# A decoder layer on one core: half of a gate block loaded inside the conditioning stream, a weight split moved ahead of a convolution, and one head's gathers reordered

## What is computed

```
mod = silu(c) @ w_ada + b_ada            # 6 x 2048: sh1, sc1, gt1, sh2, sc2, gt2
h = x * (1 + sc1) + sh1
proj = h @ w_in                          # splits: xr 2048, gr 2048, q_c 512, kv_c 512, k_r 64, g_rnn 2048, g_mla 2048
y_rnn = rg_lru(conv4(xr), gates) * gelu(gr) @ w_rnn_out
y_mla = attention(rms_norm(q_c), rms_norm(kv_c), rope(k_r)) @ w_mla_out     # 16 heads
x = layer_norm(a * x + (1 + gt1) * ((sig(g_rnn) * y_rnn + sig(g_mla) * y_mla) @ w_o))
h = x * (1 + sc2) + sh2
q = h @ peer_wq;  top 16 of 16384 experts for each of 8 heads and each token
y = sum_k gelu(h . expert_u[i_k]) * g_k * expert_v[i_k]
x = layer_norm(a * x + (1 + gt2) * y)
```

## Time and profile before

| | us |
|---|---|
| median of 3 runs | 2333.32 |
| the profiled execution's own time | 2334.12 |
| its span | 2332.4 |
| PE busy | 2073.0 (89%) |
| DVE busy | 1483.1 (64%) |
| ACT busy | 578.9 (25%) |
| POOL busy | 765.9 (33%) |
| data moved | 807.81 MB, mean 346 GB/s |

### The profile page before, as it was taken

One profiled execution on the slowest core, in us unless ns is written; L12 is line 12 of the kernel. 1 busy time (PEld: TensorE's weight loads), 2 busy tenths in 40 slices (PEclk: granted clock), 3 DMA queues, 4 the chain that ended last, 5 costly groups with the idle time before them and its releaser, 6 DMA issues.

```text
span 2332.4 us, 23238 instructions
## 1 busy us (share of the span) xinstructions
PE 2073.0 (89%) x7716; PEld 1346.1 (58%) x7716; DVE 1483.1 (64%) x2123; ACT 578.9 (25%) x1113; POOL 765.9 (33%) x764
## 2 busy tenths in 40 slices
PE   4899999999999999999987887788888899888987
PEld 3788999977888887788433333333333333333433
DVE  5746767868877556579366646665666667465444
ACT  1012553563343333221121111111111111112011
POOL 0000000011110000045465555554554554555562
PEclk7899999999999999999999889988899988989998
DMA  9976767766998675779999999999999999999996
GB/s 353 386 226 213 249 221 248 240 230 229 382 344 282 206 253 180 251 299 409 368 422 421 422 422 422 422 422 422 422 421 421 421 422 421 421 421 422 421 423 272
DMA packets 215881, 807.81 MB, mean 346 GB/s; under 512 B 24797, under 2 KB 45941, under 8 KB 149493
## 3 DMA queue, kind: packets, MB, share of 16 engines
q0 software_dynamic: 92160, 604.02, 63.5%
q1 hardware_dynamic: 122984, 202.05, 25.3%
q10 hardware_dynamic: 656, 0.66, 0.1%
HBM read 804.57 MB, written 2.10 MB: 346 GB/s over the span
## 4 chain that ended last, share of the span: by engine, by line
PE 54%; DMA 18%; DVE 11%; POOL 6%; issue 6%; ACT 4%; SPq 1%; POOLq 0%; DVEq 0%; ACTq 0%
PE ps L563 53%; DMA front<-in_peer_u,arena 15%; DVE front L1955 4%; DVE arena L1456 2%; POOL arena L504 2%; POOL front L496 1%; DMA front<-in_w_ada 1%; POOL arena L496 1%; DMA front<-in_peer_v,arena 1%; DMA arena<-in_peer_v,arena 1%; POOL arena L484 1%; POOL front L504 1%; SPq L339 1%; DMA arena<-in_w_in 1%; DVE arena L1862 0%
## 5 line engine op out<-in xcount | busy, mean ns | idle before, releaser
L563 PE MATMUL ps<-arena 128*128 128x512 f32 (+5 forms) x2798 | 967.0, 499 | 221.8 <-ACT arena L1268 182.5
L563 PEld LDWEIGHTS ps<-arena 128*128 128x128 f32 (+1 forms) x2798 | 515.5, 207 | 655.5 <-issue 467.5
L1955 DVE CUSTOM_DVE_ANT_0 front<-front,arena 128x2048 f32<-128x2048 f32 x180 | 409.3, 2292 | 199.6 <-DMA front<-in_peer_u,arena 195.5
L563 PE MATMUL ps<-front,arena 128*128 128x512 f32 (+1 forms) x832 | 355.9, 577 | 2.0 <-DMA front<-in_peer_v,arena 2.0
L1955 DVE CUSTOM_DVE_ANT_0 arena<-arena 128x2048 f32<-128x2048 f32 x60 | 137.5, 2294 | 266.2 <-DMA arena<-in_peer_u,arena 265.4
L496 POOL DMA_INDIRECT front<-in_peer_u,arena x176 | 248.5, 1412 | 68.3 <-issue 44.8
L563 PEld LDWEIGHTS ps<-front,arena 128*128 128x128 f32 x832 | 157.4, 190 | 191.1 <-issue 186.2
L1256 ACT ACTIVATE arena<-arena 128x4 f32<-128x4 f32 x64 | 13.2, 207 | 906.4 <-DVE arena L1935 906.2
L1609 DVE TENSOR_TENSOR split_ring<-front,split_pada 128x2048 fp32r<-128x2048 f32 x72 | 165.0, 2291 | 111.5 <-ACT split_pada L1147 111.1
L484 POOL COPY arena<-arena 128x4 uint32 (+1 forms) x120 | 78.2, 652 | 375.1 <-PE ps L563 350.9
L455 POOL DMA_DIRECT2D arena<-in_w_ada x64 | 34.2, 535 | 491.7 <-DVEq L1521 198.4
(11 more groups left out here) (273 smaller groups left out, 2580.8 us busy)
## 6 DMA issues: line engine op xcount, KB each, us to landing
front<-in_w_in SPq DMA_DIRECT2D x68, 1024.0 KB, 7.6
arena<-in_w_ada POOLq DMA_DIRECT2D x128, 512.0 KB, 6.2
front<-in_w_ada SPq DMA_DIRECT2D x64, 512.0 KB, 7.8
front<-in_w_rnn_out SPq DMA_DIRECT2D x16, 1024.0 KB, 6.7
front<-in_w_mla_out SPq DMA_DIRECT2D x16, 1024.0 KB, 5.2
front<-in_w_o SPq DMA_DIRECT2D x16, 1024.0 KB, 5.1
front<-in_peer_wq SPq DMA_DIRECT2D x11, 1024.0 KB, 9.8
arena<-in_w_ukv SPq DMA_DIRECT2D x16, 512.0 KB, 5.8
```

What stands on the lines that cost most here:

```text
L563: return pe.matmul(o, l, r, start=start, stop=stop, skip_group_check=True, **k)
L1955: V.tensor_tensor_reduce(uslot[s], uslot[s], h2[T], 1.0, 0.0, ALU.mult, ALU.add, zraw[:, s:s + 1]).then_inc(dots_done, 1)
```

## The change

Three parts, and two orders on ACT that belong to the first.

1. *Half a gate block in the stream.* Columns 0 to 255 of the gr block are loaded in four 512 KB pieces (`half_w`), each behind the three early units of its round, and run as `early_half(j)`, 8 matmuls into PSUM bank 5. For that the one-column sums (`ada_columns`) and the rotation of k_r move to bank 4, and stand ahead of the half. The ring then brings only columns 256 to 511, and `unit(B_XR + 1, s)` has 8 matmuls in place of 16. ACT copies the half out behind the stream, makes the square roots next and the high part of `hT` only then; the first two weights of the heads may be split earlier.
2. *First attention weights.* DVE's `head_weight(0)` moves ahead of `convolve(0)`.
3. *Third head.* The four U groups of round 2 are taken out of the loop and stand ahead of `v_group(0, 2)`, `(0, 3)`, `(1, 0)` and `(1, 1)`; the loop begins at round 2.

```diff
                 if j >= 2:
+                    sp.wait_ge(halves_used, j - 1)
+                sp.dma_start(half_w[j % 2], wv["w_in"][:, 4 * j:4 * j + 4, C_GR:C_GR + 256]).then_inc(in_head[j % 2], 16)
...
-                sp.dma_start(ring3[s], wv["w_in"][:, 4 * s:4 * s + 4, C_GR:C_GR + 512]).then_inc(in_ring[s], 16)
+                sp.dma_start(ring3[s][:, :, 256:512], wv["w_in"][:, 4 * s:4 * s + 4, C_GR + 256:C_GR + 512]).then_inc(in_ring[s], 16)
...
-            for q in (2, 3):
-                v_group(0, q)
+            for q in range(TOPK // GROUP):
+                u_group(1, 1, q)
+                v_group(*((0, q + 2) if q < 2 else (1, q - 2)))
+            v_group(1, 2)
+            v_group(1, 3)
             last = NT * PH - 1
-            with pool.Fori(1, last - 2) as H:
-                me.enter(H, 1, 2 * TOPK // GROUP)
+            with pool.Fori(2, last - 2) as H:
+                me.enter(H, 2, 2 * TOPK // GROUP)
...
-                    for m in range(4):
+                    for m in (2, 3):
                         last = mm(o[:, m, :], ring3[s][:, k, m * P:(m + 1) * P], hT[:, kt, :], kt == 0 and m % 2 == 0, kt == KT - 1)
...
+            def early_half(j):
+
+                pe.wait_ge(in_head[j % 2], 16 * (j // 2 + 1))
+                for k in range(4):
+                    kt = 4 * j + k
+                    for m in range(2):
+                        last = mm(ps[:, 5, m * S:(m + 1) * S], half_w[j % 2][:, k, m * P:(m + 1) * P], hT[:, kt, :], kt == 0 and m == 0, kt == KT - 1)
+                last.then_inc(halves_used, 1)
...
+                if j < 3:
+                    ada_columns(j + 1)
+                    early_half(j)
             last.then_inc(kr_done, 1)
             early_unit(3, 2)
+            early_half(3)
...
             low_channels(0)
+            head_weight(0)
             convolve(0)
-            head_weight(0)
```

More of the change, by code:

```diff
@@ L199, in build @@
         krw = at3(R_OT, KT, 2 * ROPE)
+        half_w = [infront(R_MODS + 3 * D + 1024 * i, 1024).rearrange("p (t c) -> p t c", t=4) for i in range(2)]
         ada_acc = at(W + 9216, 1024)
@@ L280, in build @@
         in_early = [sem(f"in_early{i}") for i in range(6)]
+        halves_used = sem("halves_used")
         in_ada = [sem(f"in_ada{i}") for i in range(3)]
@@ L303, in build @@
         keys_t, keys_ok = sem("keys_t"), sem("keys_ok")
-        var_ok, std1_ok, h2_ok, h2T_done, h2T_out = (sem(n) for n in ("var_ok", "std1_ok", "h2_ok", "h2T_done", "h2T_out"))
+        var_ok, std1_ok, h2T_done, h2T_out = (sem(n) for n in ("var_ok", "std1_ok", "h2T_done", "h2T_out"))
         sc_done, sc_out, stage_ok, best_ok, gexp_ok, topk_ok, zero_ok = (sem(n) for n in (
@@ L350, in _ @@
                     sp.dma_start(early_w[3 * (j % 2) + c], wv["w_in"][:, 4 * j:4 * j + 4, col:col + 512]).then_inc(in_early[3 * (j % 2) + c], 16)
+                if j >= 2:
+                    sp.wait_ge(halves_used, j - 1)
+                sp.dma_start(half_w[j % 2], wv["w_in"][:, 4 * j:4 * j + 4, C_GR:C_GR + 256]).then_inc(in_head[j % 2], 16)
                 if j == 0:
@@ L528, in _ @@
                     v_group(H, q)
-            me.leave(last - 3)
+            me.leave(last - 4)
             u_group(last - 1, 0, 0)
@@ L586, in unit, with ada_columns @@
                     kt = 4 * s + k
-                    for m in range(4):
+                    for m in (2, 3):
                         last = mm(o[:, m, :], ring3[s][:, k, m * P:(m + 1) * P], hT[:, kt, :], kt == 0 and m % 2 == 0, kt == KT - 1)
                 last.then_inc(unit_used, 1)
+            def early_half(j):
[5 more added lines that the diff above has]
+                last.then_inc(halves_used, 1)
+            def ada_columns(j):
+                pe.wait_ge(acc_ok, j + 1)
+                for h in range(2):
+                    for k in range(4):
+                        o = S + 8 * j + 4 * h + k
+                        last = mm(ps[:, 4, o:o + 1], acc[:, j, h, k * P:(k + 1) * P], ones[:, 0:1], j == 0 and h == 0 and k == 0, True)
+                last.then_inc(modc_done, 1)
             def early_unit(j, c):
@@ L602, in _ @@
             pe.wait_ge(xT_out, KT // 2)
+            ada_columns(0)
             for j in range(4):
[L604 to L608, removed]
                 pe.wait_ge(hT_ok, 4 * j + 4)
@@ L613, in _ @@
                 for kt in range(4 * j, 4 * j + 4):
-                    last = mm(ps[:, 4, 0:S], krw[:, kt, :], hT[:, kt, :], kt == 0, kt == KT - 1)
+                    last = mm(ps[:, 4, 0:S], krw[:, kt, :], hT[:, kt, :], False, kt == KT - 1)
+                if j < 3:
+                    ada_columns(j + 1)
+                    early_half(j)
             last.then_inc(kr_done, 1)
             early_unit(3, 2)
+            early_half(3)
             pe.wait_ge(kr_out, 1)
-            mm(ps[:, 5, 0:S], cst[:, K_ROT:K_ROT + P], krraw, True, True).then_inc(krot_done, 1)
+            mm(ps[:, 4, 0:S], cst[:, K_ROT:K_ROT + P], krraw, True, True).then_inc(krot_done, 1)
             for i in range(2):
@@ L629, in _ @@
             for g in range(4):
-                if g == 2:
+                if g == 1:
                     pe.wait_ge(std_ok, 2)
@@ L646, in queries @@
                 b = h % 2
-                pe.wait_ge(in_head[b], 32 * (h // 2 + 1))
+                pe.wait_ge(in_head[b], 32 * (h // 2 + 2))
                 if h and h % 4 == 0:
@@ L1043, in _ @@
             channels_out(B_XR, infront(XR, 1024))
-            act.wait_ge(hT_ok, KT)
-            A(S_HT[0], at(S_HT[2], KT * S), ACT.Copy).then_inc(shi_ok, 1)
+            act.wait_ge(halves_used, 4)
+            A(infront(GR, 512), ps[:, 5, :], ACT.Copy)
             for i in range(2):
@@ L1048, in _ @@
                 A(rs2[i], ps[:, 6 + i, 0:S], ACT.Sqrt, bias=eps_rms, scale=1.0 / RANK).then_inc(std_ok, 1)
+            act.wait_ge(hT_ok, KT)
+            A(S_HT[0], at(S_HT[2], KT * S), ACT.Copy).then_inc(shi_ok, 1)
             for g in range(4):
@@ L1055, in head_weight @@
                 act.wait_ge(in_ring[s], 16 * (b + SLOT_BASE))
-                act.wait_ge(unit_used, 4 * b + s - 1)
+                if i == 0:
+                    act.wait_ge(q_done, 4)
+                else:
+                    act.wait_ge(unit_used, 4 * b + s - 1 if i > 1 else 4 * B_XR + 5)
                 if i == 26:
@@ L1066, in _ @@
             head_weight(1)
-            channels_out(B_XR + 1, infront(GR, 1024))
+            act.wait_ge(unit_used, 4 * (B_XR + 2))
+            A(infront(GR + 512, 512), ps[:, 3, :], ACT.Copy).then_inc(out_act, 1)
             def output(h):
@@ L1463, in _ @@
                 dve.wait_ge(xT_out, KT // 2)
-                me.do(TT(sh1, ps[:, 5, 0:4], modc[:, 4 * j:4 * j + 4], ALU.add))
-                me.do(TT(sc1, ps[:, 5, 4:8], modc[:, KT + 4 * j:KT + 4 * j + 4], ALU.add))
+                me.do(TT(sh1, ps[:, 4, S + 8 * j:S + 8 * j + 4], modc[:, 4 * j:4 * j + 4], ALU.add))
+                me.do(TT(sc1, ps[:, 4, S + 8 * j + 4:S + 8 * j + 8], modc[:, KT + 4 * j:KT + 4 * j + 4], ALU.add))
                 me.wait()
@@ L1482, in _ @@
             me.do(TT(rt, krraw, cosT, ALU.mult))
-            me.do(TT(krT, ps[:, 5, 0:S], sinT, ALU.mult))
+            me.do(TT(krT, ps[:, 4, 0:S], sinT, ALU.mult))
             me.wait()
```

## The result

| | before | after |
|---|---|---|
| median, us | 2333.84 (5 runs, 2332.66 to 2338.18) | 2348.04 (5 runs, 2346.64 to 2355.31) |
| the profiled execution | 2334.12 | 2355.31 |
| its span | 2332.4 | 2353.6 |

The changed kernel takes 1.0061 times as long (95% interval 1.0045 to 1.0076): it is **slower by some 14 us**, where 11 us less were forecast.

The account below looks back on a forecast made before the run. It took PE's dense stretch up to the experts, then DMA at 422 GB/s, as the bounds. Stream -4.0 and POOL -6.9 gave -10.9: 2323.2 us for the profiled execution, 2322.4 as median, range 2317.5 to 2328.

Parts of the forecast that it names:

- The stream, -4.0 forecast: PE's entry into the heads: 4.7 for three half loads, 1.8 and 3.5 for halves on PE, -14.0 from ring units.
- the second edit: First head weight split ahead of the convolution: avoids 3.3 us of PE waiting for DVE, and nothing beyond.
- POOL, -6.9 forecast: Start of the experts: U gathers issued earlier fill the 25 us from 1125 that ran at 306 GB/s, gaining 6.9 us.
- so the engines stay full: Experts, from 1117: four U gathers, then the second U group from 1132, keep the DMA engines without a hole.
- a sign of being wrong: Wrong if last sums come at 130, first head unit after 210, or the hole comes back at another place.
- 55 us of 79.5: Experts: PE's products for a round take 55 us of the 79.5 that 32 gathers take at 422 GB/s.
- the V group at 1214: Queue thinnest before v_group(1, 3), with 2 us of work left; a hole of 1 to 2 us would leave 5.
- it recovers: PE in the experts makes up for V of round 0, group 3 landing late behind four U gathers.
- The V group put at 1159: V of round 0, group 3, forecast to land at 1159 in place of 1152.8, behind four U gathers.
- The reorder does nothing: Rival, 8%: gather holes only move to V groups behind U groups waiting for dots; only -4.0 remains, 2329.3 us.
- the clock stays low: Rival, 3%: PE stays at 1.2 GHz from 136 to the heads, +60 - 10.9, 2382 us.
- The thin spot at 1214: Gather queue before v_group(1, 3), 2 us of work left; a hole of 1 to 2 us was thought possible.

Follow-up runs that it names:

- e1: The change without its third part (halves and earlier first weight, gathers in old order): 2332.05 us against 2334.35 for the kernel before, ratio 0.9988.
- e8: The change's first two parts, with only round 2's first U group ahead of round 0's last two V groups: 2327.33 us, ratio 0.9971 to before.
- e7: Kernel before with only round 2's first U group moved ahead of round 0's last two V groups: 2332.39 us against 2334.64, ratio 0.9991.
- e6: Kernel before with the halves in the stream alone, first weight behind the convolution, old gathers: 2335.08 us, ratio 1.0007.
- e4: The whole change, with ACT's copy of the fourth modulation row moved behind round 1 of its expert loop: 2328.09 us, ratio 0.9974 to before.
- e2: Kernel before with the new order of the gathers alone: 2352.66 us, ratio 1.0081.
- e11: Stream part, U groups one and two ahead of v_group(0, 2) and (0, 3) respectively, ACT's modulation copy at its old place: 2336.22 us, ratio 1.0008 to before.
- e12: Control: stream part, U groups one and two ahead of v_group(0, 2) and (0, 3) respectively, ACT's modulation copy behind round 1: 2324.18 us, ratio 0.9959 to before.
- e3: Kernel before with the gather reorder, but round 2's fourth U group behind v_group(1, 1) and v_group(1, 2): 2337.15 us, ratio 1.0014.
- e5: Kernel before with only ACT's copy of the fourth modulation row moved behind round 1 of its loop: 2333.74 us, ratio 0.9999.
- e10: Stream part, U groups one and two ahead of v_group(0, 2) and (0, 3) respectively, ACT's modulation copy behind round 1: 2325.18 us, ratio 0.9964 to before.
- e9: Stream part, only round 2's first U group ahead of round 0's last V groups, ACT's modulation copy behind round 1: 2327.92 us, ratio 0.9975 to before.

## Why the prediction was wrong

**The stream, -4.0 forecast.** Right in its steps. Three halves moved DVE's round 3 by 4.04 us in place of 4.7, 1.35 us each: runs of 1 KB went like the stream's own of 2 KB. The first head unit came 3.6 us earlier in after and 4.9 in e1; over all traces it starts between 211.50 and 212.67 in the five kernels without the part and between 206.82 and 209.29 in the eight that have it together with the second edit, 3.7 us apart in the mean. At the end the part is worth 2.3 us by e1's medians, with an interval of 0.7 to 4.9 that takes the forecast in, and 5.1 by e8 against e7. The Trainium skill ("DMA: Bandwidth & Descriptors", Measured) asks for at least 1 MiB a transfer, and by its figure for 64 KB a half was put at an estimated 3.8 us. The trace does not agree: these loads of 512 KB, queued behind others, took 1.35 us each.

**The second edit, worth the 3.3 us that DVE would otherwise cost.** Right: 3.11 us of wait in e6, 3.0 us between the medians of e1 and e6.

**POOL, -6.9 forecast.** The step that failed is the sentence "so the engines stay full". The hole was filled as priced, and came back at another place, which the prediction had named as a sign of being wrong. The prediction followed the gathers only to the second U group, and asked of the rest just whether bytes and products balance (55 us of 79.5). It took for granted that the dots which free the slots of the fourth U group follow as soon as their gathers land, and never asked what stands ahead of them in DVE's order. The row was there: before, DVE began round 3's top-k at 1172.24 behind ACT's L1234, and in the new order POOL wants the slots from 1160 on (1202.50 - 42.32). The one weak place that the prediction named was the V group at 1214, and not this wait of 42.32 us. A second step held only in part: "it recovers". The V group put at 1159 came at 1160.20, but the delay reached ACT's copy as 10.6 us and was then part of the long wait.

**The rivals.** "The reorder does nothing: the holes only move, to where V groups wait behind U groups that wait for dots" had the right mechanism, at 8%, and the wrong size: it was priced at giving back the 6.9 us, while nothing bounded it there. A wait for dots lasts as long as its longest chain, here up to ACT and PE: 42.32 us on POOL, and with what followed 27.4 us of the engines' time. The case that ended on the slow side (the clock stays low, 3%) did not happen. So the sign was missed because a moved hole was priced as if it could be no deeper than the hole it replaces. The thin spot at 1214 was real: once the copy was out of the way it appeared, worth 5.0 us (e4) where 1 to 2 were named.

**Settled and open.** e2 gives the whole loss by the reorder alone, e4 and e11 against e12 take it away or put it back by moving one copy on ACT. Open is the share that comes from PE being 10.6 us later at the modulation matmuls and the share from the copy's place; no run put the matmuls elsewhere, and none put DVE's dots ahead of its top-k. An estimate from the rows: had the copy been made at 1169.90 as before, POOL would have gone on some 10.6 us sooner, and 31.7 of its 42.3 us of waiting would be left, so the place is the larger share. Open too is what e3 would give with the copy moved: its hole stands around a V group, and not at a wait for dots.

## What to carry to other kernels

Before gathers are put ahead in a queue, write down for each moved one what frees its slot, and follow that back over every engine's own order until it ends at something that is already done; a wait that costs nothing before (ACT's 30.63 us) can be the one that decides after. The price of a wait that may appear follows from the length of that chain, not from the size of the gap that is closed. And when work is moved earlier on one engine, look for copies that nobody waits for yet (here one that could come a round later at no cost, e5) that stand in program order ahead of what is now urgent on another. The Trainium skill, "Perfetto Trace Analysis", Tensor Engine Instruction, says that ACT, DVE and GpSimd take their instructions strictly in order. The trace agrees: the V group behind the waiting U group was issued only from 1213.86 on, though the products of round 0, which free its slots, were over before the modulation matmuls that let ACT's copy start at 1180.53.

## What the runs showed of the hardware

PE's clock drops for short stretches in the middle of dense work, and where it does so differs from one execution to the next. Windows of after:

```profile
367.00:370.40 3.40, 3.40 (x29) 3.30 (x29) 3.12 (x6) 1.68 (x5) 0.00 (x0) 1.00 0.72 273
370.40:373.80 3.40, 3.40 (x18) 3.40 (x17) 3.36 (x10) 0.00 (x0) 0.00 (x0) 0.50 0.02 7
455.70:459.10 3.40, 3.40 (x17) 3.40 (x17) 3.40 (x7) 0.90 (x4) 0.00 (x0) 0.51 0.24 89
```

PE is busy throughout, yet the granted clock falls to 0.50 (1.2 GHz), and 18 records run in the time of 29. Each such stretch costs some 1.5 us: three copies out of PSUM (ACT, L1147 in after, L1114 before) start at 357.45 against 361.03 in front of the first stretch, 380.55 against 382.65 behind it and 488.56 against 489.15 behind the second, so that after leads by 3.6, 2.1 and 0.6 us. Most of what it had won at 209 us is gone. The kernel before has none at these two places, nor have e2, e4, e5, e8, e10 and e12; e1, e3, e6, e7, e9 and e11 have one or both. The Trainium skill, "TensorE: Matmul & The Clock Gate", What's actually happening, has the low clock as the idle state that activity releases. No idle stretch of PE stands ahead of these: in the 40.4 us ahead of the first, PE is busy for 39.76.

The order of the instructions does not explain it. e8 and e9 run the same instructions up to the experts, yet ACT's last copy of 128x1024 scores ahead of them starts at 1099.67 in e8 and at 1106.49 in e9, where it is 1104.78 before; e3 and e7, which are the kernel before up to there, have it at 1103.36 and 1106.84. What brings the stretches on was not tried. For a reader of profiles it means that a single trace can be several us off ahead of the experts, and that a gain of a few us there has to be read from the median of many runs.
